# Output projection of the local layers: rows in another order, three units open together, weights and operands split earlier

## The reference, cut to what matters

```python
n = rmsnorm(h, attn_norm[l])
u, v_sgu, q, k, v_att = split(n @ w_in[l])          # 5 x 512 columns
u = gelu(u); v_sgu = gelu(v_sgu)
y_sgu = u * (spatial mix of rmsnorm(v_sgu))         # 4 tiles of 128 channels
y_att = rmsnorm(diff_attention(q, k, v_att))        # 4 heads of 128 channels
h = h + concat([y_sgu, y_att]) @ w_out[l]           # the output projection
h = h + conv_ffn(rmsnorm(h, ffn_norm[l]), ...)
```

## Time and profile before

| | before |
|---|---|
| time, median of 3 runs | 3593.41 us (3592.55 to 3593.98) |
| the profiled execution | 3595.14 us |
| its span from first to last instruction | 3593.2 us |
| PE busy | 3420.8 us (95%) |
| DVE busy | 1970.3 us (55%) |
| ACT busy | 1138.6 us (32%) |
| POOL busy | 347.4 us (10%) |
| mean granted clock of TensorE | 0.98 |

### The profile page before, as it was taken

The page is one execution under the profiler, slowest core; times in us unless marked ns, Lnnn a source line. Parts: engine busy times, 40 slices in busy tenths (PEclk is TensorE's granted clock), DMA queues, the critical chain, the costliest instruction groups (busy, mean ns, idle before and its releaser), DMA issues.

```text
span 3593.2 us, 47374 instructions
## 1 busy us (share of the span) xinstructions
PE 3420.8 (95%) x17388; PEld 2756.9 (77%) x17388; DVE 1970.3 (55%) x3028; ACT 1138.6 (32%) x1687; POOL 347.4 (10%) x298
## 2 busy tenths in 40 slices
PE   7999998989999999999897999999899999989999
PEld 5888766777888788876677788876778887668887
DVE  6663446666652466344666665446666624756642
ACT  4222334433221222233442322233343313343321
POOL 1000100141000100010014100011100011120002
PEclk9999999989999999999998999999999999999999
DMA  8553222104543355322210354321223332122332
GB/s 320 196 180 103 86 77 77 42 11 142 188 133 107 124 193 188 107 87 68 81 45 6 131 197 136 107 85 59 66 82 99 104 103 70 57 67 94 99 104 83
DMA packets 100385, 386.48 MB, mean 108 GB/s; under 512 B 11086, under 2 KB 12238, under 8 KB 99624
## 3 DMA queue, kind: packets, MB, share of 16 engines
q1 hardware_dynamic: 100264, 384.82, 32.5%
HBM read 382.65 MB, written 2.12 MB: 107 GB/s over the span
## 4 chain that ended last, share of the span: by engine, by line
PE 87%; DVE 7%; ACT 3%; issue 2%; DMA 1%; POOL 1%; SPq 0%; ACTq 0%; DVEq 0%; POOLq 0%
PE bank L2786 19%; PE bank L2788 19%; PE bank L2787 19%; PE bank L2891 4%; PE bank L2893 4%; PE bank L2892 4%; PE bank L2797 1%; PE bank L2798 1%; PE bank L2799 1%; ACT wH L1092 1%; DVE wL L1610 1%; PE bank L2979 1%; DMA ada<-in_ada_first 1%; PE bank L3248 1%; PE bank L2996 1%
## 5 line engine op out<-in xcount | busy, mean ns | idle before, releaser
L1092 ACT ACTIVATE wH<-wR 128x1024 fp32r<-128x1024 f32 (+2 forms) x489 | 545.5, 1116 | 1730.1 <-PE bank L2788 1382.6
L1610 DVE TENSOR_TENSOR wL<-wR,wH 128x1024 fp32r<-128x1024 f32 (+2 forms) x489 | 645.0, 1319 | 704.8 <-ACT wH L1092 704.6
L2786 PE MATMUL bank<-hH,wH 128*128 128x512 f32 x2048 | 796.8, 389 | 0.4 <-DVE wL L1610 0.4
L2787 PE MATMUL bank<-hH,wL 128*128 128x512 f32 x2048 | 796.7, 389 | 0.0
L2788 PE MATMUL bank<-hL,wH 128*128 128x512 f32 x2048 | 796.7, 389 | 0.0
L2786 PEld LDWEIGHTS bank<-hH,wH 128*128 128x128 f32 x2048 | 384.4, 188 | 80.5 <-DVE wL L1610 0.8
L2788 PEld LDWEIGHTS bank<-hL,wH 128*128 128x128 f32 x2048 | 384.4, 188 | 80.0
L2787 PEld LDWEIGHTS bank<-hH,wL 128*128 128x128 f32 x2048 | 384.4, 188 | 79.8
L2788 PE MATMUL bank<-gL,wH 128*128 128x512 f32 x1056 | 410.8, 389 | 0.0
L2786 PE MATMUL bank<-gH,wH 128*128 128x512 f32 x1056 | 410.8, 389 | 0.0
L2787 PE MATMUL bank<-gH,wL 128*128 128x512 f32 x1056 | 410.8, 389 | 0.0
(11 more groups left out here) (442 smaller groups left out, 4055.8 us busy)
## 6 DMA issues: line engine op xcount, KB each, us to landing
wR<-in_ffn_w SPq DMA_DIRECT2D x176, 512.0 KB, 3.6
adaw<-in_ada_w SPq DMA_DIRECT2D x144, 512.0 KB, 4.2
wR<-in_ffn_w SPq DMA_DIRECT2D x64, 704.0 KB, 4.1
wR<-in_w_up SPq DMA_DIRECT2D x88, 512.0 KB, 3.5
wR<-in_w_mix SPq DMA_DIRECT2D x76, 512.0 KB, 3.5
wR<-in_w_down SPq DMA_DIRECT2D x32, 704.0 KB, 4.1
wR<-in_w_in SPq DMA_DIRECT2D x40, 512.0 KB, 3.5
wR<-in_w_out SPq DMA_DIRECT2D x16, 512.0 KB, 3.5
```

The lines of the kernel that those rows point to most:

```text
L1092: act.activation(wH[n][:, 0:tiles, :], wR[n][:, 0:tiles, :], ACT.Copy).then_inc(S.w_hi, 1)
L1610: dve.tensor_tensor(wL[n][:, 0:tiles, :], wR[n][:, 0:tiles, :], wH[n][:, 0:tiles, :].bitcast(F32), ALU.subtract).then_inc(S.w_lo, 1)
L2786: pe.matmul(o, wH[n][:, k, :], rH[:, r, :], start=start and k == 0, stop=False)
L2787: pe.matmul(o, wL[n][:, k, :], rH[:, r, :], start=False, stop=False)
```

## The change

The eight row tiles of y are taken in the order attention heads 0, 1, 2, then the four u tiles, then head 3 (`Y2_TILES`, `Y2_ROWS`). The splits of y no longer go to `hH` and `hL` after the input projection, which these still serve, but to tiles that are free by then (`Y2_SPLIT`), and they are steps of the table: `y_split` of head 0 at (15, 0), of head 1 at (17, 3), of head 2 at (19, 2); the second weight unit is split into `third` at (19, 1); three of the GELUs come at (19, 1), three u x v products at (19, 2), their splits at (19, 3). PE opens units 0 and 1 over rows 0 to 6 of the new order, then unit 2 over rows 0 to 3, waits for the last y tile, and closes units 0, 1 and 2; units 3 to 7 follow one by one. The order of buffers and banks is written out (`OUT2_W`, `OUT2_BANK`, `OUT2_FREED`, `OUT2_ADDED`). The number of matmuls, splits, GELUs, table loads and additions is the same. The call `y_turn(3)` at the end of `mixers2` on PE stands where it stood, ahead of `out2`.

```diff
+Y2_TILES = (QY, QY + 1, QY + 2, QU, QU + 1, QU + 2, QU + 3, QY + 3)
+Y2_ROWS = (4, 5, 6, 0, 1, 2, 3, 7)
+Y2_SPLIT = ((QQ, QK_), (QQ + 1, QK_ + 1), (QQ + 2, QK_ + 2), (40, 41), (42, 43), (QQ + 3, QK_ + 3))
+OUT2_W = (0, 2, 1, 0, 2, 1, 0, 1)
+OUT2_FREED = (-1, -18, 0, 1, 2, 3, 4, 6)
+OUT2_BANK = (0, 1, 2, 1, 0, 1, 0, 1)
+OUT2_ADDED = (0, 0, 0, 2, 1, 4, 5, 6)
@@ places2
+    for h, (p, q) in enumerate(((15, 0), (17, 3), (19, 2))):
+        put(p, q, "y_split", h)
+    put(19, 1, "out_third")
+    put(19, 1, "gelu_u")
+    put(19, 2, "u_mul")
+    put(19, 3, "u_split")
@@ ACT, step2
+                elif name == "y_split":
+                    act.wait_ge(S.o_v, at(S.o_v, 3 * k[0] + 3))
+                    y_high(k[0])
+                elif name == "out_third":
+                    out_high(1)
+                elif name == "gelu_u":
+                    for g in range(3):
+                        gelu_u(g)
+                elif name == "u_split":
+                    for g in range(3):
+                        act.wait_ge(S.mix_y, at(S.mix_y, g + 1))
+                        y_high(3 + g)
+            def y_high(i):
+                act.activation(YH2[i], pm[:, Y2_TILES[i], :], ACT.Copy).then_inc(S.y_hi, 1)
+            def out_high(m):
+                act.wait_ge(S.w_in[m % 2], at(S.w_in[m % 2], 16 * ((V_OUT + m) // 2 + 1)))
+                act.wait_ge(S.w_used, at(S.w_used, V_OUT + OUT2_FREED[m]))
+                act.activation(W3[OUT2_W[m]][0][:, 0:KT, :], wR[m % 2][:, 0:KT, :], ACT.Copy).then_inc(S.w_hi, 1)
@@ ACT, mixers2
-                        if q == 3:
+                        if q == 3 and p < N_IN2 - 1:
...
-                hi_third(V_OUT + 2)
-                for g in range(4):
-                    act.wait_ge(S.pm, at(S.pm, landed2(QU + g)))
-                    act.activation(pm[:, QU + g, :], pm[:, QU + g, :], ACT.Gelu_apprx_tanh).then_inc(S.gelu, 1)
+                out_high(2)
+                gelu_u(3)
                 log_exp()
+                act.wait_ge(S.mix_y, at(S.mix_y, 4))
+                y_high(6)
                 y_root(3)
...
+                act.wait_ge(S.o_v, at(S.o_v, 12))
+                y_high(7)
+                for m in range(3, KT):
+                    out_high(m)
+                hi(V_UP, V_UP // 2 + 1, KT, 0)
@@ DVE
+            def y_low(i):
+                dve.wait_ge(S.y_hi, at(S.y_hi, i + 1))
+                dve.tensor_tensor(YL2[i], pm[:, Y2_TILES[i], :], YH2[i].bitcast(F32), ALU.subtract).then_inc(S.y_lo, 1)
...
                 attend(19)
-                lo_third(V_OUT + 2)
+                u_mul(3)
+                out_low(2)
+                y_low(6)
                 y_reduce(3)
...
                 y_scale(3)
-                for k in range(4):
-                    y_lo(k)
                 y_out(3)
-                for k in range(4, KT):
-                    y_lo(k)
+                y_low(7)
+            def mix_out2():
+                for m in range(KT - 1):
+                    if m:
+                        out_low(m + 2) if m + 2 < KT else lo(V_UP, KT, 0)
+                    dve.wait_ge(S.w_used, at(S.w_used, V_OUT + m + 1))
+                    dve.scalar_tensor_tensor(xT[:, m, :], bank[OUT2_BANK[m]][:, :], gate[:, m:m + 1], xT[:, m, :],
+                                             ALU.mult, ALU.add).then_inc(S.x_new, 1)
...
@@ PE
+                pe.wait_ge(S.w_lo, at(S.w_lo, V_OUT + 2))
+                for i in range(KT - 1):
+                    pe.wait_ge(S.y_lo, at(S.y_lo, i + 1))
+                    for m in range(2):
+                        rows(m, i, i + 1)
+                pe.wait_ge(S.w_lo, at(S.w_lo, V_OUT + 3))
+                pe.wait_ge(S.s_max, at(S.s_max, 32))
+                rows(2, 0, 4)
+                pe.wait_ge(S.y_lo, at(S.y_lo, KT))
+                for m in range(2):
+                    rows(m, KT - 1, KT)
+                rows(2, 4, KT)
+                for m in range(3, KT):
+                    pe.wait_ge(S.w_lo, at(S.w_lo, V_OUT + m + 1))
+                    pe.wait_ge(S.x_new, at(S.x_new, OUT2_ADDED[m]))
+                    rows(m, 0, KT)
...
                 mixers2((S.h_lo, 0))
-                project(V_OUT, KT // 2, S.x_new, 0, (S.y_lo, 0))
+                out2()
```

More of the change, by code:

```diff
@@ L681, in build @@
         RTM = [pmv(f"RTM{i}", 42 + i, [P, T]) for i in range(2)]
+        YH2 = [pmv(f"YH2{i}", t[0], [P, T], F32R)[:, :] for i, t in enumerate(Y2_SPLIT)] + [hH[:, 6, :], hH[:, 7, :]]
+        YL2 = [pmv(f"YL2{i}", t[1], [P, T], F32R)[:, :] for i, t in enumerate(Y2_SPLIT)] + [hL[:, 6, :], hL[:, 7, :]]
+        W3 = ((wH[0], wL[0]), (wH[1], wL[1]), third)
         VA = [pm[:, QA + h, :].rearrange("p (t c) -> p t c", t=TT) for h in range(4)]
@@ L1497, in step2, with gelu_u @@
                     y_root(*k)
+                elif name == "y_split":
[12 more added lines that the diff above has]
+                act.activation(YH2[i], pm[:, Y2_TILES[i], :], ACT.Copy).then_inc(S.y_hi, 1)
+            def gelu_u(g):
+                act.wait_ge(S.pm, at(S.pm, landed2(QU + g)))
+                act.activation(pm[:, QU + g, :], pm[:, QU + g, :], ACT.Gelu_apprx_tanh).then_inc(S.gelu, 1)
+            def out_high(m):
+                act.wait_ge(S.w_in[m % 2], at(S.w_in[m % 2], 16 * ((V_OUT + m) // 2 + 1)))
+                act.wait_ge(S.w_used, at(S.w_used, V_OUT + OUT2_FREED[m]))
+                act.activation(W3[OUT2_W[m]][0][:, 0:KT, :], wR[m % 2][:, 0:KT, :], ACT.Copy).then_inc(S.w_hi, 1)
             def steps2(p, q):
@@ L2449, in y_out, with u_mul, out_low @@
                                   ALU.mult).then_inc(S.o_v, 1)
-            def y_lo(k):
-                dve.wait_ge(S.y_hi, at(S.y_hi, k + 1))
-                dve.tensor_tensor(hL[:, k, :], pm[:, Y2_TILES[k], :], hH[:, k, :].bitcast(F32), ALU.subtract).then_inc(S.y_lo, 1)
+            def y_low(i):
+                dve.wait_ge(S.y_hi, at(S.y_hi, i + 1))
+                dve.tensor_tensor(YL2[i], pm[:, Y2_TILES[i], :], YH2[i].bitcast(F32), ALU.subtract).then_inc(S.y_lo, 1)
+            def u_mul(g):
+                dve.wait_ge(S.gelu, at(S.gelu, 4 + g + 1))
+                y = pm[:, QU + g, :]
+                dve.tensor_tensor(y, y, pm[:, QV + g, :], ALU.mult).then_inc(S.mix_y, 1)
+            def out_low(m):
+                dve.wait_ge(S.w_hi, at(S.w_hi, V_OUT + m + 1))
+                high, low = W3[OUT2_W[m]]
+                dve.tensor_tensor(low[:, 0:KT, :], wR[m % 2][:, 0:KT, :], high[:, 0:KT, :].bitcast(F32),
+                                  ALU.subtract).then_inc(S.w_lo, 1)
             def step2(name, *k):
@@ L2488, in step2 @@
                     y_out(*k)
+                elif name == "y_split":
+                    y_low(k[0])
+                elif name == "out_third":
+                    out_low(1)
+                elif name == "u_mul":
+                    dve.wait_ge(S.mix_b, at(S.mix_b, 4))
+                    for g in range(3):
+                        u_mul(g)
+                elif name == "u_split":
+                    for g in range(3):
+                        y_low(3 + g)
             def steps2(p, q):
@@ L2507, in mixers2 @@
                             keep(p)
-                            lo(V_IN + p + 2, KT, p % 2)
+                            if p < N_IN2 - 1:
+                                lo(V_IN + p + 2, KT, p % 2)
                         steps2(p, q)
                 attend(19)
-                lo_third(V_OUT + 2)
+                u_mul(3)
+                out_low(2)
+                y_low(6)
                 y_reduce(3)
[L2513 to L2517, removed]
                 y_scale(3)
-                for k in range(4):
-                    y_lo(k)
                 y_out(3)
-                for k in range(4, KT):
-                    y_lo(k)
+                y_low(7)
[6 more added lines that the diff above has]
+                                             ALU.mult, ALU.add).then_inc(S.x_new, 1)
+                dve.wait_ge(S.w_used, at(S.w_used, V_OUT + KT))
+                add_last(OUT2_BANK[KT - 1], 0)
+                split_second(V_UP + 1)
             def up2(ubase, next_tiles):
@@ L2554, in layer2 @@
                 mixers2()
-                project_out(V_OUT, 0, KT)
+                mix_out2()
                 norm(1, 1)
@@ L3467, in up2, with out2, rows @@
                     turn(i)
+            def out2():
+                def rows(m, i0, i1):
+                    wh, wl = W3[OUT2_W[m]]
+                    o = bank[OUT2_BANK[m]][:, :]
+                    for i in range(i0, i1):
+                        k = Y2_ROWS[i]
+                        pe.matmul(o, wh[:, k, :], YH2[i], start=i == 0, stop=False)
+                        pe.matmul(o, wl[:, k, :], YH2[i], start=False, stop=False)
+                        mm = pe.matmul(o, wh[:, k, :], YL2[i], start=False, stop=i == KT - 1)
+                    if i1 == KT:
+                        mm.then_inc(S.w_used, 1)
+                pe.wait_ge(S.w_lo, at(S.w_lo, V_OUT + 2))
```

(1 more changed line is left out.)

9 lines of the change are left out of this document (removed).

## The result

The changed kernel took 3611.45 us (median of 6 runs, 3609.8 to 3615.14), the kernel before in the same runs 3593.69 (6 runs, 3592.4 to 3595.16): a ratio of 1.0049, 95% interval 1.0039 to 1.006. That is 17.8 us slower, where 13.4 were forecast and 3600.0 to 3612.7 was the range. The profiled execution took 3610.22, its span is 3608.3 us, so between the two profiled executions the spans differ by 15.1.

The account below looks back on a forecast made before the run. PE, busy 95% of the span, was taken as the bound. Per layer 2.6 + 1.6 + 2.1 - 0.3 = 6.0 us, twice 12.0, plus 1.4 of clock: 13.4 slower, 3606.8 us, range 3600.0 to 3612.7.

Parts of the forecast that it names:

- PE has to pass `y_turn(3)` first: Behind unit 19: PE, in order, cannot multiply ready rows during the 7.94 us wait; no gain from the new row order.
- (c): Rival at the projection: PE need not pass y_turn(3) first; 5.4 us per layer gained, 3582.5 us; chance 0.03.
- The round trip at (15, 0): DVE's low part of head 0 waits for ACT's copy; PE loses 2.6 us more per layer, 3.3 in all.
- (a): Rival: round trips at (15, 0) and (17, 3) hidden, only 1.8 us per layer counts, 3597.0 us; chance 0.10.
- (17, 3): Split of head 1: DVE waits for ACT again, AD comes 2.0 us later, 1.6 us per layer reach PE.
- The tail: From unit 19 to y_turn(3): three products and the splits delay head 3's scaling, 2.1 us more per layer.
- (b): Rival behind unit 19: products and GELUs done in time, POOL's square overlaps; 3.1 us per layer gained, 3587.2; chance 0.05.
- The bank for unit 2: Addition before the third unit: unit 2's own bank removes a 0.26 us wait, taken as 0.3 us off per layer.
- the thin cover: Behind unit 0: unit 3's split and two additions take 3.1 us against 15 matmuls, 3.4 us; if gone, tenths lost.
- a wait on unit 3's bank: Sign of a wrong prediction: PE waiting again on unit 3's split or bank, which was costed at nothing.
- The clock: Behind the 3.3 us wait at (16, 0): 3 us at half clock, 1.4 us lost, taken once in two layers.
- (d): Rival: half-clock stretches at (16, 0) and (19, 0) in both layers, 12.0 + 5.6 us, 3611.0 us; chance 0.12.

Follow-up runs that it names:

- Head 3 first: Changed kernel, DVE and ACT doing head 3's sum, root, scaling before the fourth product and unit 2's split: 3573.61 us with the turn moved, 3587.45 with it in place.
- the kernel without round trips: Changed kernel with ACT's copies of heads 0 and 1 moved ahead of an earlier group of exponentials, DVE's splits left in place: 3601.46 us.
- `y_turn(3)` late: Changed kernel with y_turn(3) moved behind the first four row tiles of unit 2, and unit 1 in a bank of its own: 3592.83 us.
- before with two round trips: Kernel before plus an unused ACT copy and DVE subtraction at (15, 0) and at (17, 3): 3607.15 us, ratio 1.0034.
- before with one: Kernel before plus an unused ACT copy and DVE subtraction at (15, 0) alone: 3602.57 us, ratio 1.0023.

## Why the prediction was right, and what was mis-sized

**PE has to pass `y_turn(3)` first: right.** No row tile of the projection started in the 9.81 us. Moving this one call gave 18.6 us, so the rival by which the change does what its name says (c) fell by the order of PE's program alone, and its mechanism is real: it only was not in the change. Its price was not met. With the call moved the kernel is level with before (3592.83 against 3594.44) and not 10.9 us under it, because the last tile then costs a wait of 2.29 us and the clock at (16, 0) stands against it, neither of which (c) counted.

**The round trip at (15, 0): right.** 2.6 us more, 3.3 in all; measured 3.30 in both layers, and 3.33 and 3.30 in the kernel before with nothing but this trip. DVE's wait was 1.90 us. The rival of hidden trips (a) fell: taking them away gained 10.0 us.

**(17, 3): right.** 1.6 taken, 1.42 and 1.43 seen as a wait, 1.6 by the difference of the two stretches.

**The tail: nearly right.** 2.1 taken, 1.87 measured. Unit 19's copy is at 2564.44, while its last matmul begins at 2561.77: it starts 2.3 us behind that matmul's end (2562.16), as forecast, so the rival of a shorter tail (b) fell. POOL's square did run to the end of DVE's three instructions and 0.89 beyond. By the Trainium skill (SBUF — State Buffer, "SBUF: two separate sides") a DVE instruction with two SBUF inputs and a GpSimd one that reads SBUF share one port pair as an exclusive lock: the one that starts first has it for its whole instruction, and the other waits. The trace agrees, as the square took 3.15 us against 1.04 alone, and with one DVE split or with three it ended 0.89 to 0.90 us behind the last of them. Head 3 first shows that the tail is a matter of order: the same instructions in another order, and 4.43 us of wait against 9.82 in the kernel without round trips.

**The bank for unit 2: wrong, small.** 0.3 us less was taken; PE waited 0.40 us there instead of 0.26. It is unit 3's addition, of the thin cover that the prediction named: the cost moved, it did not go. The prediction had named a wait on unit 3's bank as a sign that it was wrong, and this sign came true, at the tenths that it put on it.

**The clock: the mis-sized term.** The prediction took 1.4 us once in the two layers, from a stretch of 3 us at half clock. It came in both layers at (16, 0), and cost 2.60 and 1.25 us in the profiled execution, 3.85 in all, since in the first layer it lasted some 6 us and not 3; at (19, 0), with 1.42 us of rest, it did not come. This is 2.5 us of the miss. Rival (d) is nearest in its time, 3611.0, but half of its stretches didn't occur. That the measured time lies in the range, 1.25 us below its upper end, is therefore luck in part: this end is (d) and 1.7 us more for the profiled execution, which lay below its median this time.

**The sum.** For the steps within the two stretches the forecast was 14.0 us (6.3 twice, and 1.4); they measured 16.1: 2.45 more of clock, 0.46 less in the tail, 0.35 less at (17, 3), 0.5 in smaller steps. With the bank and the -1.0 outside, the span was forecast 13.4 longer and came out 15.1, a miss of 1.7. The other 2.7 of the 4.4 between 13.4 and 17.8 are where the profiled executions lie: before's 1.45 above the median of its 6 runs, after's 1.2 below its own. A longer half-clock stretch in the second layer of the other executions is no likely source: the other three kernels with the same rest at (16, 0) (`y_turn(3)` late, before with two round trips, before with one) lost 2.59 to 2.64 us in the first layer and 1.25 to 1.26 in the second when they were profiled. What makes up the 2.7 stays open.

## What to carry to other kernels

A split in two instructions on two engines, put between two steps that feed the bound engine, makes one in-order queue wait for the other; give the first half at least one earlier place in its queue, and put the second behind the last instruction that the bound engine waits for. When work is to fill a wait, look in the bound engine's own program whether the waiting instruction stands ahead of it, and after filling, look at what the filler had covered. And charge a new wait of the matmul engine with the clock behind it: here 3.3 us of wait cost up to 2.6 more.

## What was unexpected of the hardware

Behind a rest of 3.30 us TensorE ran at 1.2 GHz for some 6 us in the first layer and some 3.5 in the second, so the price of the same wait differs within one execution (2.60 and 1.25 us), and it does so in the same way in all four kernels that have this rest. Behind rests of 1.32 and 1.42 us it stayed at 2.4 GHz in both layers. Behind one of 2.29 us it stayed there in the first layer and fell to 1.2 GHz in the second; behind 2.41 us it fell in both. Why the same rest is followed by different stretches no run here shows. Idle matmuls in the rest kept the clock at 2.4 GHz.

GpSimd's square of 128x512 took 1.04 us alone, 1.42 or 1.95 with one split of DVE beside it, and 3.15 with three back to back. It ended 0.89 to 0.90 us behind the last of them each time: with three it did not finish in between, although DVE's instructions are separate ones.
